# Stages behind a layer norm that open on raw inputs: four outputs before the norm is known, scale and bias put on the results

## The chip, the cores and the metric

The kernel runs on one NeuronCore of a Trainium2 chip. The metric is the device time of one execution in microseconds (us). TensorE (PE) multiplies, VectorE (DVE), ScalarE (ACT) and GpSimd (POOL) work on tiles in SBUF and in the PSUM banks; SyncE (SP) issues the DMAs.

## The reference, cut

Two transformer blocks of two layers each stand behind one another. Features are 1024 wide, there are 256 tokens in the first block and 272 (16 meta tokens ahead) in the second. Every layer norm is followed by the projections of the next part, which read its result `u` and nothing else:

```python
def layer_norm(x, g, b):
    mu = jnp.mean(xf, -1, keepdims=True)
    var = jnp.mean(jnp.square(xf - mu), -1, keepdims=True)
    return (xf - mu) * lax.rsqrt(var + EPS) * g + b
def swiglu(x, w_gate, w_up, w_down):
    return (jax.nn.silu(x @ w_gate) * (x @ w_up)) @ w_down
# first block, layer i (mixer 0 is RWKV-7, mixer 1 a gated delta net, "gdn")
    x = _layer_norm(DEEPNORM_ALPHA * x + (1 + ga1) * y, ln_g[i, 0], ln_b[i, 0])
    u = x * (1 + sc2) + sh2
    gate, up = jnp.split(u @ ffn_w_in[i], 2, axis=-1)
    y = (jax.nn.silu(gate) * up) @ ffn_w_out[i]
    x = _layer_norm(DEEPNORM_ALPHA * x + (1 + ga2) * y, ln_g[i, 1], ln_b[i, 1])
# second block, layer l
    h = layer_norm(ALPHA * h + 0.5 * swiglu(h, ffn1...), ln1_g[l], ln1_b[l])
    proj = h @ w_in[l]                      # SSD, forgetting and latent attention
    h = layer_norm(ALPHA * h + mix, ln2_g[l], ln2_b[l])
    h = layer_norm(ALPHA * h + 0.5 * swiglu(h, ffn2...), ln3_g[l], ln3_b[l])
```

Everything is fp32. The factor and summand on each norm's result that lead to `u` (g and b, and for the first block the modulation too) are kept as `lnc[:, n, 0, j]` and `lnc[:, n, 1, j]`, n the norm and j the tile of 128 features; `lnc[:, n, 2]` and `[3]` are those of the residual base (ALPHA times the norm's result).

## The kernel before

**Stages.** Behind the first mixer nine stages run: `STAGES = ("ffn", "gdn", "ffn", "ffn", "mixer", "ffn", "ffn", "mixer", "ffn")`, numbered 0 to 8, with norm n ahead of stage n (stage 3 opens the second block) and norm 9 at the end. Tiles are features by tokens: 8 tiles of 128 features, T = 256 or 272 columns. A ffn has 22 hidden tiles f, each with a gate output and an up output; outputs go to PSUM banks, gate f to bank 2(f%3), up f to the next one.

**Precision.** A product of fp32 numbers is made of three products on high and low parts (fp32r): high weight by high input, low weight by high input, high weight by low input. At 256 columns the high and low input stand side by side, so that one product 512 wide does two of them (f of 2 and more), and the halves are added behind it (`HALF`, `half_out`, L1929).

**Weights.** The weights come as slabs of 1 MB (16 blocks of 128x128) through a `ring` of 5 slots. ScalarE makes the high part into `high` (3 slots, L1446). Then the low part goes to `ring_low` by `ring - high`: on GpSimd (L2485) or, for hidden tiles of a ffn, on VectorE (`low_by_vector_engine`, L1909). `STAGE_AT[n]` (q0 below) is the stage's first slab.

**The norm.** `residual` (VectorE, ScalarE) takes the output projection's banks, adds them to the residual tiles `XAS` (L1829, L1832), subtracts a `shift` (half the mean over tiles that were early, kept in bank 3) into arena slot 9 (`less_shift`, L1810), and ScalarE squares them (L1434). The squares of tiles 1 to 6 go to PSUM banks 1 and 2, and VectorE adds them up (`add_square`, L1816). TensorE sums over features with matrix `con` into bank 4 (mean) and bank 5 (mean square). `norm` on VectorE (L1854 to L1901): variance, centering of XAS by pairs of tiles (`center`, L1858), ScalarE's square root, the reciprocal (L1868), then for each tile `normed_tile` (L1873), the whole input with scale and bias (L1888) and its low part (L1896, `input_low`); ScalarE's `norm_out` makes the input's high part (L1471, `input_high_ready`). Behind the eighth low part VectorE writes the residual base of eight tiles (L1901), which GpSimd sums (`base_sums`, L2501).

**The opening.** `first_four` on TensorE (all products have line L531) runs 4 outputs over k = 0 to 7, three products per output and k, 96 in all, and waits at each k for `input_high_ready` and `input_low`. In gdn and mixer stages these are the first four tiles of the convolution's channels, taken from banks 0 to 3 by VectorE's `convolve` (L2200, L2203) and ScalarE's silu (L1620, L1695); behind them stands a small product (`gdn_ba`, `dtf`) from which VectorE makes the decay rows (L2178 to L2214).

**GpSimd's order.** Its program for a stage is written out by hand:

```python
                weights_low(q0)
                weights_low(q0 + 1)
                eng.wait_ge(input_low, g.nth(input_low, DT))
                weights_low(q0 + 2)
                base_sums(To)
```

VectorE makes slab q0+3 at the start of `ffn`, and the high parts of q0+2 and q0+3 are first in ScalarE's `ffn` (in gdn and mixer stages q0+2 stands behind the norm).

## Time and profile before

| | us |
|---|---|
| median of 3 runs | 2307.1 |
| lowest, highest | 2302.41, 2310.05 |
| the profiled execution | 2305.64 |
| its span in the trace | 2303.7 |

In the span PE is busy 2112.9 us, DVE 1224.2, ACT 869.2 and POOL 708.9. The mean granted clock of TensorE is 0.958 of full speed. A row of the timeline shows the start, the duration with merged repeats (x2 is two instructions in a row), the engine and line, and in square brackets how long the engine had been idle and which instruction it was that ended this. Matmuls overlap, so durations of one are longer than the distance of two starts.

### The profile page before, as it was taken

The numbers are of one execution on the slowest core, as the hardware profiler recorded it, in microseconds if no ns is written. First come the engines' busy times: TensorE is split into PE (matmuls) and PEld (weight loads), VectorE is DVE, ScalarE is ACT, GpSimd is POOL, SyncE is SP. The second block draws the span as 40 slices with busy tenths as digits, with TensorE's granted clock in tenths as the row PEclk, the third lists the DMA queues.
The fourth block names the chain that finished last, engine by engine and source line by source line (L and its number), as shares of the span: only waits on it lengthen the run. The fifth ranks groups of instructions, "written<-read, shape, count | busy, mean of one in ns | idle before, by whom it ended". The sixth has DMA issues, their size and how long they took to land.

```text
span 2303.7 us, 40612 instructions
## 1 busy us (share of the span) xinstructions
PE 2112.9 (92%) x17634; PEld 1904.4 (83%) x17634; DVE 1224.2 (53%) x2205; ACT 869.2 (38%) x1258; POOL 708.9 (31%) x316
## 2 busy tenths in 40 slices
PE   4989988999988989999999898899999998989997
PEld 3867866889887867898999895699989997857897
DVE  6166445763673347653642666555264418457652
ACT  0442111454443223543433444343343334434543
POOL 0350001314573003126314560131561175304124
PEclk9998998999999899999999998899999998979999
DMA  8564442455343003554444340245435453304552
GB/s 330 220 274 148 149 163 75 150 184 188 141 147 128 2 1 128 188 196 166 160 170 180 131 147 19 92 169 180 167 145 179 169 177 108 119 19 147 184 191 83
DMA packets 49681, 340.43 MB, mean 148 GB/s; under 512 B 6368, under 2 KB 8416, under 8 KB 8672
## 3 DMA queue, kind: packets, MB, share of 16 engines
q1 hardware_dynamic: 49504, 337.84, 40.6%
q8 instruction: 139, 2.28, 0.4%
q14 instruction: 38, 0.31, 0.0%
HBM read 336.77 MB, written 1.05 MB: 147 GB/s over the span
## 4 chain that ended last, share of the span: by engine, by line
PE 81%; DVE 12%; ACT 3%; issue 2%; POOL 1%; DMA 1%; SPq 0%; ACTq 0%; POOLq 0%; DVEq 0%
PE bank L531 80%; POOL ring_low L2485 1%; DMA ada_ring<-ada 1%; DVE arena L1873 1%; DVE arena L1901 1%; PE bank L537 1%; DVE arena L1858 1%; ACT high L1446 1%; DVE small L1868 1%; DVE arena_parts L1896 1%; DVE arena L1888 0%; DVE ZZ L2082 0%; DVE small L2340 0%; DVE small L2451 0%; DVE acc L1963 0%
## 5 line engine op out<-in xcount | busy, mean ns | idle before, releaser
L531 PE MATMUL bank<-arena_parts,high 128*128 128x272 f32 (+2 forms) x4512 | 1026.4, 315 | 61.2 <-ACT arena_parts L1471 38.0
L531 PEld LDWEIGHTS bank<-arena_parts,high 128*128 128x128 f32 x4512 | 749.8, 191 | 111.6 <-issue 48.8
L531 PE MATMUL bank<-arena_parts,ring_low 128*128 128x272 f32 (+2 forms) x2736 | 782.1, 288 | 0.0
L1446 ACT ACTIVATE high<-ring 128x2048 fp32r<-128x2048 f32 x237 | 453.1, 1914 | 679.5 <-PE bank L531 593.5
L2485 POOL TENSOR_TENSOR ring_low<-ring,high 128x2048 fp32r<-128x2048 f32 x105 | 485.3, 4626 | 697.3 <-ACT high L1446 697.3
L531 PEld LDWEIGHTS bank<-arena_parts,ring_low 128*128 128x128 f32 (+1 forms) x2736 | 523.7, 191 | 1.0
L1909 DVE TENSOR_TENSOR ring_low<-ring,high 128x2048 fp32r<-128x2048 f32 x132 | 303.6, 2300 | 181.1 <-ACT high L1446 181.1
L531 PE MATMUL bank<-hidden_high,high 128*128 128x256 f32 (+1 forms) x1056 | 303.2, 287 | 0.0
L531 PE MATMUL bank<-hidden_low,high 128*128 128x256 f32 (+1 forms) x1056 | 301.1, 285 | 0.0
L531 PE MATMUL bank<-hidden_high,ring_low 128*128 128x256 f32 (+1 forms) x1056 | 300.1, 284 | 0.0
L2485 POOL TENSOR_TENSOR hidden_low<-arena,hidden_high 128x256 fp32r<-128x256 f32 (+1 forms) x132 | 111.8, 849 | 575.4 <-DVE hidden_high L1925 575.4
L531 PE MATMUL bank<-arena,ring 128*128 128x256 f32 (+2 forms) x992 | 230.6, 394 | 28.5 <-DVE arena L2158 7.8
L531 PEld LDWEIGHTS bank<-arena,ring 128*128 128x128 f32 (+1 forms) x992 | 192.9, 195 | 63.1 <-issue 11.4
L531 PEld LDWEIGHTS bank<-hidden_high,high 128*128 128x128 f32 x1056 | 199.0, 188 | 0.5
L531 PEld LDWEIGHTS bank<-hidden_high,ring_low 128*128 128x128 f32 x1056 | 198.9, 188 | 0.4
L531 PEld LDWEIGHTS bank<-hidden_low,high 128*128 128x128 f32 x1056 | 199.0, 188 | 0.0
L1829 DVE SCALAR_TENSOR_TENSOR acc<-bank,acc 128x272 f32<-128x272 f32 (+1 forms) x42 | 18.3, 436 | 177.8 <-PE bank L531 177.8
L531 PE MATMUL bank<-arena,con 64*64 64x64 f32 (+7 forms) x532 | 88.4, 336 | 15.7 <-issue 7.3
L531 PEld LDWEIGHTS bank<-arena,con 64*64 64x64 f32 (+4 forms) x532 | 45.4, 145 | 54.8 <-issue 24.8
L2501 POOL TENSOR_TENSOR acc<-arena 128x256 f32<-128x256 f32 (+1 forms) x20 | 26.9, 1345 | 194.9 <-PE bank L531 187.3
L1929 DVE TENSOR_TENSOR bank<-AZ,bank 128x256 f32<-128x256 f32 x60 | 25.8, 429 | 108.9 <-ACT AZ L1486 108.9
L2529 POOL TENSOR_TENSOR acc<-acc,ada_ring 128x1024 f32<-128x1024 f32 x21 | 49.6, 2363 | 99.4 <-ACT ada_ring L1458 97.4
(327 smaller groups left out, 2262.7 us busy)
## 6 DMA issues: line engine op xcount, KB each, us to landing
ring<-stream SPq DMA_DIRECT2D x269, 1024.0 KB, 4.8
ada_ring<-ada SPq DMA_DIRECT2D x48, 1024.0 KB, 6.2
con<-consts SPq DMA_DIRECT2D x1, 1542.5 KB, 11.1
con<-consts SPq DMA_DIRECT2D x1, 1040.0 KB, 7.2
arena<-xin SPq DMA_DIRECT2D x1, 1024.0 KB, 11.9
out<-arena SPq DMA_DIRECT2D x2, 512.0 KB, 2.9
prob_even<-consts SPq DMA_DIRECT2D x1, 320.0 KB, 11.4
par<-params SPq DMA_DIRECT2D x1, 272.5 KB, 9.7
```

Source lines behind the costliest of these rows:

```text
L531: ins = nc.tensor.matmul(o, l, r, start=start, stop=stop_, skip_group_check=True)
L537: ins = nc.tensor.transpose(o, x, con[0:rows, CC["ident"]:CC["ident"] + rows])
L1446: act(high[:, q % HIGHS], ring[:, s % RING], ACT.Copy).then_inc(a.sig(high_ready), 1)
L1858: nv.tensor_tensor(x, x, over_tiles(bank[4][:, 0:T], 2, T), ALU.subtract).then_inc(v.sig(vstep), 1)
L1868: nv.reciprocal(small[:, 2, 0:T], small[:, 1, 0:T]).then_inc(v.sig(vstep), 1)
L1873: nv.tensor_tensor(tl(9, j, T), tl(XAS, j, T, t0), small[:, 2, 0:T], ALU.mult).then_inc(v.sig(normed), 1)
L1896: nv.tensor_tensor(input_rest(j, T), tl(US, j, T, t0), input_high(STAGES[n], j, T).bitcast(F32), ALU.subtract).then_inc(v.sig(input_low), 1)
L1909: nv.tensor_tensor(ring_low[:, HL[q] % RING], ring[:, HL[q] % RING], high[:, q % HIGHS].bitcast(F32), ALU.subtract).then_inc(low_by_vector, 1)
L1929: nv.tensor_tensor(bank[b][:, 0:T], HALF[:, 0], bank[b][:, SEQ:], ALU.add).then_inc(v.sig(gate_added), 1)
L2485: ng.tensor_tensor(out, whole, part, ALU.subtract).then_inc(signal, 1)
L2501: ng.tensor_tensor(s_, first, tl(XAS, j, T, t0), ALU.add).then_inc(g.sig(sums_ready if j == 6 else pool_step), 1)
L2529: ng.tensor_tensor(acc[:, n % 2], acc[:, n % 2], w_k, ALU.add).then_inc(g.sig(ada_used if k % 2 else pool_step), 1)
```

## The change

Eight stages (`OPENED_RAW`, all but 3) open otherwise. Let x' be the tile less the shift (slot 9), g the gain, m the mean that remains in x', s the reciprocal of the deviation. With W the weight, W(g (x' - m) s + b) = s (W(g x') - m Wg) + Wb. So the four first outputs run on g x' (`raw_high` by ScalarE's `raw_tile`, `raw_low` by VectorE's `raw_rest`) before m and s are known. Four more columns per tile, the high and low parts of g and b (`raw_columns`), give Wg and Wb in the same products. The two norm sums (`mean_sum`, `square_sum`) move into the opening's k = 0. Then `scale_opened` on VectorE adds up the extra columns, puts -m Wg on the bank, multiplies by s, and (gdn and mixer) adds Wb. In a ffn, Wb of the gate is the bias of ScalarE's silu, and Wb of up is added in the hidden tile's instruction. The normed tiles are needed from the fifth output on (f=2), or by the small product.

With it go: `center` works on slot 9 with the mean in SBUF (`small[:, 0]`), one pair ahead of each pair of normed tiles; `less_shift` of tiles 4 to 7 reads the shift from SBUF (`small[:, 1]`); squares go to SBUF (`staged`) and not to banks 1, 2; the residual base is a function of its own and moves behind f=1 (ffn) or behind conv 2 (gdn, mixer), and in stage 3 to the start of `ffn`; ScalarE makes the high part of q0+2 before the first normed tile's high part and that of q0+3 in quarters behind tiles 2 to 5; GpSimd makes the low parts of q0 to q0+3 in a row.

```diff
+OPENED_RAW = (0, 1, 2, 4, 5, 6, 7, 8)
-    return STAGES[n] == "ffn" and HIGHS <= q - STAGE_AT[n] < HIGHS + FT
+    return STAGES[n] == "ffn" and HIGHS < q - STAGE_AT[n] < HIGHS + FT
...
+            def raw_four(n, tiles, T, signals):
+                for b in range(4):
+                    eng.wait_ge(*freed(b))
+                eng.wait_ge(raw_high_ready, pe.nth(raw_high_ready, 1))
+                eng.wait_ge(raw_low_ready, pe.nth(raw_low_ready, 1))
+                for k in range(DT):
+                    eng.wait_ge(raw_high_ready, pe.nth(raw_high_ready))
+                    eng.wait_ge(raw_low_ready, pe.nth(raw_low_ready))
+                    both, low = raw_both(n, k, T), raw_low(n, k, T)
...
+                    for b, (w_high, w_low) in enumerate(blocks):
+                        if k == 0 and b == 2:
+                            mean_sum(T)
+                        mm(bank[b][:, 0:T + 4], w_high, both, k == 0, False)
+                        m = mm(bank[b][:, 0:T + 4], w_low, both, False, k == DT - 1, hold=k == DT - 1)
+                    if k == 0:
+                        square_sum(T)
+                    if k < DT - 1:
+                        for b, (w_high, w_low) in enumerate(blocks):
+                            m = mm(bank[b][:, 0:T], w_high, low, False, False, hold=b == 3)
+                        m.then_inc(opened, 1)
+            def normal_tile():
+                eng.wait_ge(input_high_ready, pe.nth(input_high_ready))
+                eng.wait_ge(input_low, pe.nth(input_low))
...
         @block.scalar
-                    to = bank[1 + j % 2][:, 0:T] if j else square_sums(T)
+                    to = staged[:, j % 2, 0:T] if j else square_sums(T)
                     act(to, tl(9, j, T), ACT.Square).then_inc(a.sig(squared), 1)
+                    if raw:
+                        raw_tile(n, j, T)
                     if j >= 5 and highs:
                         weights_high(highs[j - 5])
...
+            def norm_out(n, T):
+                weights_high(STAGE_AT[n] + 2)
                 for j in range(DT):
                     eng.wait_ge(normed, a.nth(normed))
+                    act(input_high(STAGES[n], j, T), tl(9, j, T), ACT.Identity, ...)
+                    if raw and 2 <= j < 6:
+                        quarter_high(STAGE_AT[n] + HIGHS, j - 2)
...
         @block.vector
+            AFTER_FFN = ({5: (0, 1, 2), 6: (3, 4, 5, 6)}, ((), (), (7,)))
+            AFTER_MIXING = ({5: (0, 1), 6: (2,)}, ((3,), (4, 5), (6, 7)))
...
-                    nv.tensor_tensor(tl(9, j, T), tl(XAS, j, T, t0), bank[3][:, 0:T], ALU.subtract)
+                    shift = bank[3] if j < 4 else small[:, 1]
+                    nv.tensor_tensor(tl(9, j, T), tl(XAS, j, T, t0), shift[:, 0:T], ALU.subtract)
-                    nv.tensor_tensor(squares, squares, bank[1 + j % 2][:, 0:T], ALU.add)
+                    nv.tensor_tensor(squares, squares, staged[:, j % 2, 0:T], ALU.add)
...
-                    x = arena[:, XAS, 2 * q:2 * q + 2, t0:t0 + T]
-                    nv.tensor_tensor(x, x, over_tiles(bank[4][:, 0:T], 2, T), ALU.subtract)
+                    x = arena[:, 9, 2 * q:2 * q + 2, 0:T]
+                    nv.tensor_tensor(x, x, over_tiles(small[:, 0, 0:T], 2, T), ALU.add)
...
+            def scale_opened(b, T, signal, to_bias):
+                both = bank[b][:, T:T + 4].rearrange("p (a e) -> p a e", e=2)
+                nv.tensor_reduce(opening_cols[:, b], both, AX_X, ALU.add)
+                for i in range(1 if to_bias else 2):
+                    nv.scalar_tensor_tensor(out=product, in0=small[:, i, 0:T], scalar=opening_cols[:, b, i:i + 1], in1=product, ...)
+                nv.tensor_tensor(product, product, small[:, 2, 0:T], ALU.mult)
...
         @block.gpsimd
                 weights_low(q0)
                 weights_low(q0 + 1)
-                eng.wait_ge(input_low, g.nth(input_low, DT))
                 weights_low(q0 + 2)
+                weights_low(q0 + 3)
                 base_sums(To)
```

GpSimd, at the boundary to stage 0, before the change (`acc` rows are the sums of the residual base):

```order
L2501 TENSOR_TENSOR acc<-acc,arena 128x256 [waits pool_step]
L2485 TENSOR_TENSOR ring_low<-ring,high 128x2048 [waits weights_high_ready] x2
L2485 TENSOR_TENSOR ring_low<-ring,high 128x2048 [waits weights_high_ready,input_low]
L2501 TENSOR_TENSOR acc<-arena 128x256 [waits residual_base_ready]
```

and with it:

```order
L2688 TENSOR_TENSOR acc<-acc,arena 128x256 [waits pool_step]
L2672 TENSOR_TENSOR ring_low<-ring,high 128x2048 [waits weights_high_ready] x4
L2688 TENSOR_TENSOR acc<-arena 128x256 [waits residual_base_ready]
L2688 TENSOR_TENSOR acc<-acc,arena 128x256 [waits pool_step] x2
```

The third slab no longer waits for `input_low`, and a fourth one, which was VectorE's, stands behind it.

VectorE at the same place, from the last residual tile on, before (L1832 the last tile, L1810 `less_shift`, L1868 the reciprocal):

```order
L1832 SCALAR_TENSOR_TENSOR arena<-bank,mod,arena 128x256
L1810 TENSOR_TENSOR arena<-arena,bank 128x256
L1854 TENSOR_TENSOR small<-bank,small 128x256
L1858 TENSOR_TENSOR arena<-arena,bank 128x2x256
L1864 SCALAR_TENSOR_TENSOR small<-bank,small 128x256
L1858 TENSOR_TENSOR arena<-arena,bank 128x2x256
L1868 RECIPROCAL small<-small 128x256
L1873 TENSOR_TENSOR arena<-arena,small 128x256 x2
L1888 TENSOR_SCALAR arena<-arena,lnc 128x256 x2
L1858 TENSOR_TENSOR arena<-arena,bank 128x2x256 x2
L1896 TENSOR_TENSOR arena_parts<-arena,arena_parts 128x256 x2
```

and with the change (L1932 is `raw_rest`, L2003 `center`, L2013 `normed_tile`):

```order
L1966 SCALAR_TENSOR_TENSOR arena<-bank,mod,arena 128x256
L1944 TENSOR_TENSOR arena<-arena,small 128x256
L1932 SCALAR_TENSOR_TENSOR arena_parts<-arena,lnc,arena_parts 128x256
L1991 TENSOR_TENSOR small<-small,bank 128x256
L1932 SCALAR_TENSOR_TENSOR arena_parts<-arena,lnc,arena_parts 128x256 x2
L1996 SCALAR_TENSOR_TENSOR small<-bank,small 128x256
L1932 SCALAR_TENSOR_TENSOR arena_parts<-arena,lnc,arena_parts 128x256 x2
L2003 TENSOR_TENSOR arena<-arena,small 128x2x256
L2008 RECIPROCAL small<-small 128x256
L2013 TENSOR_TENSOR arena<-arena,small 128x256 x2
L2031 TENSOR_SCALAR arena<-arena,lnc 128x256 x2
L2003 TENSOR_TENSOR arena<-arena,small 128x2x256
```

Five `raw_rest` instructions now stand among them, one `center` less stands ahead of the reciprocal, and `less_shift` and `center` read `small`, not a bank.

## Rows read from the trace of the kernel before

**Rows 1.** The page, busy time (share) xinstructions, and the chain by engine.

```profile
PE 2112.9 (92%) x17634; PEld 1904.4 (83%) x17634; DVE 1224.2 (53%) x2205; ACT 869.2 (38%) x1258; POOL 708.9 (31%) x316
...
PE 81%; DVE 12%; ACT 3%; issue 2%; POOL 1%; DMA 1%; SPq 0%; ACTq 0%; POOLq 0%; DVEq 0%
```

**Rows 2.** PE's waits: instruction <- releaser: us in total, times, longest.

```profile
PE bank L531 <- ACT arena_parts L1471: 38.0, 9, 4.3
...
PE bank L531 <- ACT arena L1695: 8.8, 4, 2.4
...
PE bank L531 <- POOL ring_low L2485: 7.2, 8, 1.1
```

**Rows 3.** Timeline of PE: start, us, instruction [idle before <-releaser], first norm.

```profile
406.53 0.59 PE L531 MATMUL bank<-acc,con 128*128 128x256 f32 x2
...
413.02 0.55 PE L531 MATMUL bank<-arena_parts,high 128*128 128x256 f32 x1 [4.15 <-ACT arena_parts L1471]
...
427.31 0.47 PE L531 MATMUL bank<-arena_parts,high 128*128 128x512 f32 x1 [0.81 <-POOL ring_low L2485]
...
444.16 0.39 PE L531 MATMUL bank<-arena_parts,high 128*128 128x512 f32 x1
```

**Rows 4.** Windows: us, PE busy (matmuls), granted clock, DMA share, GB/s.

```profile
413.02:417.20 4.18, 4.18 (x19) 0.50 0.53 198
417.20:427.30 10.10, 9.30 (x79) 1.00 0.35 128
...
609.30:615.30 6.00, 5.98 (x28) 0.50 0.01 3
```

**Rows 5.** Timeline of DVE, first norm, its first and last steps.

```profile
411.71 0.76 DVE L1873 TENSOR_TENSOR arena<-arena,small 128x256 f32<-128x256 f32 x2
...
420.19 0.76 DVE L1896 TENSOR_TENSOR arena_parts<-arena,arena_parts 128x256 fp32r<-128x256 f32 x2
```

**Rows 6.** Lines (ns min/median/max); timeline of DVE and POOL behind the first norm.

```profile
L1901 DVE TENSOR_SCALAR arena<-arena,lnc x72: 396/423/4868, 420.9 to 2114.3; 128x256 f32<-128x256 f32 x40, 128x272 f32<-128x272 f32 x32
...
L2189 DVE SCALAR_TENSOR_TENSOR arena<-arena x21: 411/428/4730, 647.7 to 1950.6; 12x272 f32<-12x272 f32 x14, 8x256 f32<-8x256 f32 x7
...
L2180 DVE RECIPROCAL arena<-arena x3: 1740/1841/1842, 640.7 to 1941.9; 12x272 f32<-12x272 f32 x2, 8x256 f32<-8x256 f32 x1
...
L1810 DVE TENSOR_TENSOR arena<-arena,bank x80: 409/421/439, 395.9 to 2290.2; 128x256 f32<-128x256 f32 x48, 128x272 f32<-128x272 f32 x32
...
421.51 6.46 DVE L1901 TENSOR_SCALAR arena<-arena,lnc 128x256 f32<-128x256 f32 x6
...
422.38 4.79 POOL L2485 TENSOR_TENSOR ring_low<-ring,high 128x2048 fp32r<-128x2048 f32 x1 [25.87 <-ACT high L1446]
```

**Rows 7.** Timeline of POOL and DVE, residual phase behind the first feed-forward.

```profile
594.52 9.17 POOL L2485 TENSOR_TENSOR ring_low<-ring,high 128x2048 fp32r<-128x2048 f32 x2 [2.61 <-ACT high L1446]
...
595.25 0.42 DVE L1810 TENSOR_TENSOR arena<-arena,bank 128x256 f32<-128x256 f32 x1
```

**Rows 8.** Prices: POOL's group (busy, mean ns), and lines (ns min/median/max).

```profile
L2485 POOL TENSOR_TENSOR ring_low<-ring,high 128x2048 fp32r<-128x2048 f32 x105 | 485.3, 4626 | 697.3 <-ACT high L1446 697.3
...
L1446 ACT ACTIVATE high<-ring x237: 1892/1917/1927, 356.7 to 2272.1; 128x2048 fp32r<-128x2048 f32 x119
...
L1909 DVE TENSOR_TENSOR ring_low<-ring,high x132: 2273/2287/2781, 427.9 to 2228.8; 128x2048 fp32r<-128x2048 f32 x132
...
L2203 DVE SCALAR_TENSOR_TENSOR XX<-bank,par,XX x72: 479/482/486, 626.2 to 698.7; 128x255 f32<-128x255 f32 x24, 128x254 f32<-128x254 f32 x24, 128x253 f32<-128x253 f32 x24
...
L2366 DVE COPY TC<-bank x6: 148/160/165, 1387.8 to 2001.8; 128x12 f32<-128x12 f32 x4, 16x12 f32<-16x12 f32 x2
```

**Rows 9.** Timeline of DVE and PE in the gdn stage.

```profile
617.12 7.11 DVE L1901 TENSOR_SCALAR arena<-arena,lnc 128x256 f32<-128x256 f32 x8
...
642.46 4.47 DVE L2182 TENSOR_TENSOR arena<-arena 8x256 f32<-8x256 f32 x1
...
655.14 0.58 PE L531 MATMUL bank<-arena_parts,high 128*128 128x256 f32 x1 [6.45 <-ACT arena L1620]
```

More of the change, by code:

```diff
@@ L1066, in _ @@
             out_projection("rwkv_out", 0, 8, lambda k: tl(5, k), SEQ)
-            norm(SEQ)
-            ffn("ffn_in", "ffn_in", "ffn_out", 0, SEQ, FT)
-            norm(SEQ)
-            first_four("gdn", [("gdn_in", 0, n) for n in range(4)], SEQ, [told(b, "vector") for b in B4])
+            ffn(0, "ffn_in", "ffn_in", "ffn_out", 0, SEQ, FT)
+            raw_four(1, [("gdn_in", 0, n) for n in range(4)], SEQ, [told(b, "vector") for b in B4])
             prev[0:4] = ["scalar"] * 4
@@ L1237, in mixer @@
             def mixer(l):
-                first_four("mixer", [("mix_in", l, n) for n in range(4)], T, [told(b, "vector") for b in B4])
+                raw_four(4 + 3 * l, [("mix_in", l, n) for n in range(4)], T, [told(b, "vector") for b in B4])
                 prev[0:4] = ["scalar"] * 4
@@ L1477, in ffn, with result_out @@
+                if not raw:
+                    weights_high(STAGE_AT[n] + HIGHS)
+            def result_out(n, T):
+                for j in range(DT):
+                    eng.wait_ge(normed, a.nth(normed))
+                    act(tl(US, j, T, xview(T)), tl(9, j, T), ACT.Identity, bias=lnc[:, n, 1, j:j + 1],
+                        scale=lnc[:, n, 0, j:j + 1]).then_inc(a.sig(output_ready), 1)
             def ffn(n, T):
                 q0 = STAGE_AT[n]
-                weights_high(q0 + 2)
@@ L1815, in add_square @@
                         eng.wait_ge(*added["squares"])
-                    nv.tensor_tensor(squares, squares, bank[1 + j % 2][:, 0:T], ALU.add).then_inc(v.sig(square_added), 1)
+                    nv.tensor_tensor(squares, squares, staged[:, j % 2, 0:T], ALU.add).then_inc(v.sig(square_added), 1)
                     added["squares"] = v.last
@@ L1872, in normed_tile @@
                     eng.wait_ge(*centers[j // 2])
-                    nv.tensor_tensor(tl(9, j, T), tl(XAS, j, T, t0), small[:, 2, 0:T], ALU.mult).then_inc(v.sig(normed), 1)
+                    nv.tensor_tensor(tl(9, j, T), tl(9, j, T), small[:, 2, 0:T], ALU.mult).then_inc(v.sig(normed), 1)
                     return v.last
                 if n == len(STAGES):
-                    centers += [center(2), center(3)]
+                    centers += [center(1), center(2), center(3)]
                     for j in range(DT):
```

304 lines of the change are left out of this document (210 added, 94 removed).

## The prediction

> **What bounds the kernel now.** I read the page's busy shares and its chain first: TensorE is busy 92% of the span and carries 81% of the chain, VectorE 12% [rows 1]. So TensorE's idle time is what an edit can win. The list of TensorE's waits names the part this change aims at: nine waits for ScalarE's normed inputs (L1471), 38.0 us, and eight for GpSimd's `ring_low` (L2485), 7.2 us [rows 2]. The timeline of the first layer norm shows both: the first product of the next stage starts at 413.02 after 4.15 us idle, the third output (f=2) only at 427.31, f=5 at 444.16, so 5.62 us per output from there on [rows 3]. The windows show the clock: after the gap 4.2 us ran at 0.50 of full speed, the lower of the two levels (1.2 GHz), and 6.0 us at the second norm [rows 4]. Ten norms run, one before each of nine stages and one at the end; eight stages (all but stage 3) get the new opening.
>
> **What is freed on TensorE.** The opening is 96 products before and after. The gap ends; 96 products at the warm 0.118 us (79 records took 9.30 us in the third window [rows 4]) are 11.4 us, the four passes of norm sums now inside it 0.9. From the end of the product that closes the projection (407.1 [rows 3]) TensorE would stand before f=2 at 419.5 and not at 427.31: 7.8 us, if all inputs are there. The extra four columns (64 products 260 wide for 256) are 0.1 us per stage. Over eight stages some 60 us are on offer.
>
> **What TensorE then waits for.** f=2, and in gdn and mixer stages the small product behind the four outputs, needs the normed tiles. VectorE makes them in the order of before: its chain ran from 411.71 to 420.9 [rows 5]. Now two raw tails more stand ahead of the variance and two behind it, 0.4 us each, less the second `center`: the reciprocal ends at 412.9 and not 411.7, and with one more `center` per pair the chain would end at 422.9. TensorE, waiting for it in f=2, keeps some 3.9 of the 7.8.
>
> **The mechanism on which I decide.** VectorE instructions whose tensor inputs all lie in SBUF stop while GpSimd runs. L1901, scale and bias of a tile in SBUF, takes 0.42 us as a rule and 4.87 at most [rows 6]: six of them, due 2 us, took 6.46 from 421.51 because GpSimd's `weights_low` ran 422.38 to 427.17. A scalar_tensor_tensor on SBUF tiles waited likewise (L2189, 0.43 as a rule, 4.73 at most), and a tensor_tensor (L2182, 4.47 us for 8x256) [rows 6, 9]. The reciprocal does not: L2180 stays between 1.74 and 1.84. Nor does L1810, one input in PSUM: never over 0.439 in 80 calls, though GpSimd ran two weight slabs beside it from 594.52 [rows 6, 7]. Before, the norm's critical chain was clear of GpSimd: the third `weights_low` waited for the eighth `input_low`, and up to there VectorE's shift, centering and square sums had PSUM inputs.
> The Trainium skill, SBUF — State Buffer, "SBUF: two separate sides", states it as a rule: VectorE in a two-port mode or with two SBUF inputs and GpSimd share a port pair by an exclusive lock held for the whole instruction. L1901 (4.87) and L1810 (0.439) agree; it is a rule against this change.
>
> The change drops the wait for `input_low`, gives GpSimd a fourth slab in the opening, and takes the PSUM operands away from `less_shift` for tiles 4 to 7, `add_square` and `center`. Prices: a slab is 4.63 us on GpSimd, its high part 1.9 on ScalarE, its low part 2.29 on VectorE [rows 8].
> - Third slab. ScalarE makes its high part right after the square root (1.9 us), before VectorE's reciprocal (1.74) and the instruction ahead of it have ended. GpSimd gets the port first, from about 412.1 to 416.7; the first `normed_tile`, ready at 412.9, starts at 416.7: 3.8 us.
> - Fourth slab. ScalarE's quarters end after tile 5 (about 424.7); VectorE is in tiles 6 and 7: 4.6 us more.
> So `input_low` 8 comes at 422.9 + 3.8 + 4.6, and 0.5 for the quarters between ScalarE's tiles: 431.8, not 420.9. f=2 has idled 1, 2 and 6 us between its tiles by then; its up half runs 432.2 to 435.0 (before: to 432.9, 427.31 + 5.62).
> - Handover. VectorE scales the first gate and up after that: for each a reduce, a scalar_tensor_tensor of PSUM (0.48 [rows 8]) and a product (0.42), then two products of 0.48 and the silu: 3.5 us. The reduce of four columns has no row. Its bounds are 0 and 0.48; I take 0.12, by the copies of 12 PSUM columns, 0.16 [rows 8]. f=3 starts at 435.5 (before 432.9), f=4 at 441.6 (438.5), and, since eight `residual_base` (2.7), a 2.29 slab and the halves stand before tile 2, f=5 at 448.6 (444.16 [rows 3]). From there TensorE is the bound, so the stage keeps +4.4. At 272 columns no halves are added and an output takes longer on TensorE: of the 4.4 some 2.1 stay (stage 5).
>
> **After a feed-forward** the residual phase is hit too. GpSimd's slab starts at 594.52, and VectorE's `less_shift(6)` at 595.25 [rows 7]; with the raw tile ahead of ScalarE's high part the slab starts at 595.0. Now an SBUF instruction, `less_shift(6)` waits to 599.6; square 6, and behind it high part and slab q0+1, come 4 us later, and that slab (602.8 to 607.4) lies over `less_shift(7)`. Squares and sums are 3.7 us late. TensorE, which has the square sum behind its first eight products, idles 3 us there; then come the two slabs of above. By the same sum: stage 6 (ffn) +3.7; stage 3, without raw opening but with the new order, +4.5.
>
> **gdn (stage 1).** TensorE's tile 10 waited 6.45 us to 655.14 for a ScalarE silu behind VectorE's conv 6, which stood behind the decay rows (L2182 at 642.46 is one) [rows 9]. So VectorE's chain sets that time. Its `input_low` 8 moves from 617.1 [rows 9] by the late squares 3.7, raw tails and centers 2.2, and the two slabs 3.8 + 4.6: +14.3. Then four openings add 1.45 each to the convolutions (+5.8); `residual_base` no longer meets a slab (4.87 - 0.42 = -4.4); the decay rows meet other slabs (-4: one of their two stops of 4.0 and 4.3 falls away; 0 if neither does). Sum +11.7. **Mixers (4, 7).** The decay rows have slack there. What binds is bank 3 coming free, behind three opened convolutions, the base and a fourth: VectorE's chain +12, openings +5.8, base -4.4, less the old waits for L1695 (8.8 us in the two [rows 2], 4.4 each) and 0.5 of slack: +8.5 each. The final norm: one more `center` behind the reciprocal, +0.6 to 1.
>
> **Sum.** Stages 0, 2, 8: 3 x 4.4 = 13.2; stage 5: 2.1; stage 6: 3.7; stage 3: 4.5; stage 1: 11.7; stages 4, 7: 17; the end 0.8: **+53**. The clock gives nothing back at the boundaries counted here, since f=2 waited for GpSimd's slab in the trace of before, not for the slow products. The profiled execution took 2305.64 us for a span of 2303.7; its time plus 53 is 2358.6. The median of the three runs is 1.5 above it, so I take 2359.
>
> **The rivals.**
> 1. *The port does not decide* (faster). If GpSimd's slabs fall where VectorE is in reciprocals or PSUM work, or the stop is shorter than L1901's, what is left is the clean order. f=5 of stage 0 then starts at 440.2, 3.9 us before the old one; 3.9 x 3 for stages 0, 2, 8, stage 5 -6, stage 6 -6.5, stages 3 and 9 0, gdn and mixers +3 and +2.3 x 2 by the openings. Sum -17 with old clocks, down to -34 where the half-speed stretches of the gdn and mixer openings also go (up to 6.0 [rows 4]): 2272 to 2290. For it: the idle time of [rows 2] is real. Against it: the one L1901 of 4.8 us that each of the nine `residual_base` runs holds.
> 2. *Some of the stops miss.* The race at 595.0 against 595.25 is 0.3 us wide. If `less_shift(6)` wins in all five boundaries behind a feed-forward, some 3.5 x 5 = 17 fall away: 2341. If besides the fourth slab came after `input_low` 8 (ScalarE 7 us later), 8 x 3 more: about 2315.
> 3. *More idle brings more half-speed time.* The 6 us gap in f=2 and 3 us in k=0 are of the length that stood before 4.2 and 6.0 us at half speed [rows 3, 4]; where products, not VectorE, bind behind it, that is 1 to 2.5 us for each of nine: 2358 + 15 = 2373.
>
> **How the numbers follow.** Forecast with its variants 2 (first) and 3: 0.76. The strong form of rival 2, around 2315: 0.07. Rival 1: 0.14. The rest, 0.03, is within 0.3%, which is about what a measurement of this kernel can tell from no change (2300 to 2314), and half of rival 2's strong form lies beside its edge: 0.06 for no change in all, 0.80 slower. I leave out rival 1 and the farthest sums, so the range is 2308 to 2378. Faster by over 0.3%: 0.14.
>
> **What would show it.** In the profile after: TensorE's list without the 4.2 us waits before the opening, and in their place waits inside f=2 and the small products for VectorE's `input_low`, 5 to 7 us at the longest; the first `normed_tile` of most norms at 4 us and another one at 5 instead of 0.43; `less_shift` up to 4.5 us; GpSimd's slab starting while the reciprocal runs. It is wrong if these instructions keep 0.42 us beside a running slab, if the tile-6 `less_shift` stays short, or if gdn's tile 10 starts less than 8 us later against its projection's end.

## The result and the profile after

| | before | with the change |
|---|---|---|
| median, us | 2306.88 (4 runs, 2302.41 to 2310.05) | 2384.73 (4 runs, 2384.56 to 2385.05) |
| ratio | | 1.0344, 95% interval 1.0319 to 1.0369 |
| span of the profiled execution | 2303.7 | 2382.8 |

3.4% slower: the direction of the forecast, and outside its range (2308 to 2378). The forecast was +53 us; the profiled spans differ by 79.1.

The page of the changed kernel, busy times and the chain of work that ended last, beside [rows 1]:

```profile
PE 2130.4 (89%) x17634; PEld 1919.7 (81%) x17634; DVE 1352.5 (57%) x2386; ACT 900.2 (38%) x1362; POOL 730.0 (31%) x322
...
PE 57%; DVE 12%; issue 2%; ACT 2%; ACTq 0%; DVEq 0%
```

VectorE is busy 128 us more. A stopped instruction counts as busy. With GpSimd's opening slabs left out (`no_open_lows` and its control, below) VectorE is busy 1238.8 us in the changed kernel and 1183.2 in the one before. So some 56 us are more work (among it 64 raw tails of 0.49 us), and the time that goes with the slabs rose from 41 to 114 us. The waits of TensorE (instruction <- releaser: us in all, times, longest), beside [rows 2]:

```profile
PE bank L568 <- DVE arena_parts L2039: 63.5, 23, 5.3
...
PE bank L568 <- ACT arena L1810: 23.5, 4, 9.2
PE bank L568 <- DVE arena L1966: 19.8, 6, 5.4
```

The nine waits of 4.2 us ahead of the openings are down to one (stage 3, which opens as before). In their place stand waits for VectorE's low parts of the input (L2039), in f=2 and in the small products; for the mixers' silu (L1810); and, not forecast, for the last residual tile (L1966).

The timeline of VectorE and GpSimd behind the first norm shows the mechanism on which the forecast decided, beside [rows 5]. First VectorE, then GpSimd:

```profile
419.49 1.75 DVE L2008 RECIPROCAL small<-small 128x256 f32<-128x256 f32 x1
421.27 4.48 DVE L2013 TENSOR_TENSOR arena<-arena,small 128x256 f32<-128x256 f32 x2
...
433.43 4.60 DVE L2031 TENSOR_SCALAR arena<-arena,lnc 128x256 f32<-128x256 f32 x1
...
420.52 4.61 POOL L2672 TENSOR_TENSOR ring_low<-ring,high 128x2048 fp32r<-128x2048 f32 x1 [15.67 <-ACT high L1540]
432.83 5.05 POOL L2672 TENSOR_TENSOR ring_low<-ring,high 128x2048 fp32r<-128x2048 f32 x1 [7.70 <-ACT high L1566]
```

GpSimd's third slab starts while the reciprocal runs (which keeps its 1.75), and the first normed tile is free only when the slab ends; the fourth slab stops a whole tile (L2031) for 4.2 us. So it is in all eight raw norms: the first normed tile takes 4.0 to 4.5 us there, the whole tile 4.6. The residual phase ahead of norm 4 (behind a feed-forward) shows what the forecast had wrong:

```profile
1319.32 0.44 DVE L1944 TENSOR_TENSOR arena<-arena,small 128x272 f32<-128x272 f32 x1
1319.68 9.56 DVE L1950 TENSOR_TENSOR acc<-acc,XX 128x272 f32<-128x272 f32 x2
1329.16 1.73 DVE L1932 SCALAR_TENSOR_TENSOR arena_parts<-arena,lnc,arena_parts 128x272 fp32r<-128x272 f32 x4
1330.81 0.43 DVE L1966 SCALAR_TENSOR_TENSOR arena<-bank,arena 128x272 f32<-128x272 f32 x1
...
1319.61 9.33 POOL L2672 TENSOR_TENSOR ring_low<-ring,high 128x2048 fp32r<-128x2048 f32 x2 [5.50 <-ACT high L1540]
...
1331.30 1.27 PE L568 MATMUL bank<-arena,con 128*128 128x272 f32 x2 [4.45 <-DVE arena L1966]
```

`less_shift(6)` (L1944) just gets ahead of the slab, so ScalarE squares the tile and makes the next high part at once, and slab q0+1 follows q0 without a gap. Two `add_square` (L1950) stand still, 9.56 us for 0.87 us of work; the raw tails and the last residual tile, which TensorE waits for, stand behind them.

I set the two traces side by side stage by stage. The mark is the sixth of the eight products `bank<-acc,con` ahead of each norm (at norm 0 it starts at 405.02 in the kernel before, 1.5 us ahead of the 406.53 of [rows 3]); it stands at the same place among the 17634 products in every kernel. Stage n runs from the mark of norm n to that of norm n+1. Differences to the profiled execution of before, us:

| kernel | head | 0 | 1 | 2 | 3 | 4 | 5 | 6 | 7 | 8 | end |
|---|---|---|---|---|---|---|---|---|---|---|---|
| forecast | 0 | 4.4 | 11.7 | 4.4 | 4.5 | 8.5 | 2.1 | 3.7 | 8.5 | 4.4 | 0.8 |
| the change | 8.4 | 3.1 | 10.5 | 2.9 | 6.6 | 15.1 | 3.1 | 8.4 | 17.0 | 3.4 | 0.6 |
| changed_again | 3.8 | 3.2 | 10.6 | 2.9 | 6.6 | 19.3 | 2.7 | 8.2 | 16.8 | 3.3 | 0.6 |
| no_open_lows | 3.6 | -5.3 | -4.6 | -5.2 | -0.9 | 4.4 | -7.0 | -7.7 | -1.5 | -5.4 | 0.6 |
| no_open_lows_before | 1.7 | -0.9 | -12.7 | -1.2 | -0.9 | 0.5 | -0.4 | -1.5 | -2.9 | -1.3 | 0.0 |
| before_sbuf_operands | 6.6 | 0.2 | 3.1 | 0.3 | 2.1 | -1.9 | 0.0 | 1.2 | 1.7 | 0.1 | 0.0 |
| before_third_slab_early | 5.9 | 4.5 | -4.4 | 4.2 | 5.1 | 1.6 | 3.9 | 3.9 | -2.4 | 4.5 | 0.0 |
| changed_psum_squares | 1.9 | 2.9 | 7.3 | 2.7 | 4.0 | 15.6 | 2.7 | 5.0 | 10.2 | 3.1 | 0.6 |
| third_waits_again | 0.6 | 2.1 | 1.3 | 1.9 | 2.8 | 10.6 | 1.9 | 7.7 | 5.0 | 2.2 | 0.6 |
| second_slab_behind_shift | 2.8 | 3.1 | 7.1 | 2.9 | 4.7 | 16.3 | 3.4 | 5.3 | 13.7 | 3.4 | 0.6 |
| third_high_ahead | 3.1 | -0.6 | 15.8 | 0.0 | 7.3 | 22.9 | -0.7 | 8.3 | 24.0 | -0.3 | 0.6 |
| slabs_in_quarters | -0.4 | 2.6 | 7.5 | 2.5 | 4.3 | 15.3 | 2.3 | 4.5 | 12.1 | 2.3 | 0.6 |
| open_behind_mixers_3 | 9.6 | -4.4 | 0.8 | -4.4 | 0.9 | 1.9 | -5.7 | 0.8 | 0.4 | -4.4 | 0.6 |

Stages 0, 2, 3, 5, 6, 8 are feed-forwards, 1 is gdn, 4 and 7 are mixers. The head is the time ahead of the first mark. Its difference scatters from execution to execution: at the first residual sum of norm 0 (394.88 before), ahead of which no edit acts, the eighteen traces lie between -0.8 and +8.5. So some times below are compared without the heads too. Only where the third slab runs ahead of the first mark is a part of the head the edit's own: 1.1 us in open_behind_mixers_3, 3.9 in third_high_ahead.

### The profile page after: what moved, and what is told of

Same layout as the page of the kernel before. It is cut to its first block, busy times and chain, and to the rows that moved or that the text cites. A ratio compares the mean times of both kernels' runs of the same rounds, so it can differ in the third digit from the quotient of the medians.

```text
span 2382.8 us, 41142 instructions
## 1 busy us (share of the span) xinstructions
PE 2130.4 (89%) x17634; PEld 1919.7 (81%) x17634; DVE 1352.5 (57%) x2386; ACT 900.2 (38%) x1362; POOL 730.0 (31%) x322
## 4 chain that ended last, share of the span: by engine, by line
PE 57%; DVE 12%; issue 2%; ACT 2%; ACTq 0%; DVEq 0%
PE bank L568 56%; DVE acc L1950 2%; DVE arena L2031 2%; DVE arena L2384 1%; PE bank L574 1%; DVE arena_parts L2039 1%; DVE arena L2013 1%; DVE bank L2057 1%; DVE arena_parts L1932 0%; DVE small L2008 0%; DVE XX L2384 0%; DVE arena L2003 0%; DVE arena L2047 0%; DVE small L2638 0%; DVE small L2527 0%
## 5 line engine op out<-in xcount | busy, mean ns | idle before, releaser
L568 PE MATMUL bank<-arena_parts,high 128*128 128x272 f32 (+4 forms) x4512 | 1042.4, 318 | 102.1 <-DVE arena_parts L2039 63.5
L568 PE MATMUL bank<-arena_parts,ring_low 128*128 128x272 f32 (+4 forms) x2736 | 786.1, 290 | 0.0
L2672 POOL TENSOR_TENSOR ring_low<-ring,high 128x2048 fp32r<-128x2048 f32 x111 | 515.2, 4644 | 691.6 <-ACT high L1540 628.8
L1540 ACT ACTIVATE high<-ring 128x2048 fp32r<-128x2048 f32 x229 | 438.4, 1914 | 638.4 <-PE bank L568 551.9
L2065 DVE TENSOR_TENSOR ring_low<-ring,high 128x2048 fp32r<-128x2048 f32 x126 | 290.6, 2306 | 172.7 <-ACT high L1540 172.7
L2688 POOL TENSOR_TENSOR acc<-arena 128x256 f32<-128x256 f32 (+1 forms) x20 | 14.9, 746 | 317.9 <-PE bank L568 194.0
L568 PE MATMUL bank<-arena,con 64*64 64x64 f32 (+7 forms) x512 | 82.1, 334 | 31.7 <-DVE arena L1966 19.8
L1950 DVE TENSOR_TENSOR acc<-acc,XX 128x256 f32<-128x256 f32 (+1 forms) x60 | 76.0, 1267 | 59.6 <-ACT XX L1513 57.2
```

The lines of the kernel that those rows point to most:

```text
L568: ins = nc.tensor.matmul(o, l, r, start=start, stop=stop_, skip_group_check=True)
L1540: act(high[:, q % HIGHS], ring[:, s % RING], ACT.Copy).then_inc(a.sig(high_ready), 1)
L1950: nv.tensor_tensor(squares, squares, staged[:, j % 2, 0:T], ALU.add).then_inc(v.sig(square_added), 1)
L2065: nv.tensor_tensor(ring_low[:, HL[q] % RING], ring[:, HL[q] % RING], high[:, q % HIGHS].bitcast(F32), ALU.subtract).then_inc(low_by_vector, 1)
L2672: ng.tensor_tensor(out, whole, part, ALU.subtract).then_inc(signal, 1)
```

## The experiments

**Is it the slabs at all?** The low parts of the opening are left out, in the changed kernel and in the one before.

```diff
-                weights_low(q0)
-                weights_low(q0 + 1)
-                weights_low(q0 + 2)
-                weights_low(q0 + 3)
+                for q in range(q0, q0 + 4):
+                    eng.wait_ge(high_ready, q + 1)
+                    rest(low_stub[:, ...one column...], low_stub[:, 0:1], low_stub[:, 0:1], low_by_gpsimd)
```

In both kernels TensorE takes the high parts in place of the low parts left out, in as many products of the same size.

> The changed kernel, with GpSimd's four weights_low of each opening (q0 to q0+3) left out: GpSimd only signals, and TensorE multiplies by the high part in place of the low one, in as many products of the same size. Theory A (GpSimd's slabs stop VectorE's SBUF instructions): no normed_tile, whole tile or add_square over 1 us is left, and the time falls from 2384.7 to between 2280 and 2300. Rival B (VectorE simply has more to do: raw tails, scaling of the opened banks, one more center): the slabs are not what is waited for, the time stays above 2350.

> The kernel before, with its three weights_low of each opening left out in the same way: the control for the run above. Both theories: TensorE's eight waits for ring_low (7.2 us) and the stopped L1901 go, the rest stays: 2290 to 2302 against 2307. What this run and the one above differ in is what the change gives or costs where no slab stands in VectorE's way: theory A says -5 to -20, rival B +30 or more.

Measured: 2276.36 us for the changed kernel and 2286.04 for the one before, beside a run of before at 2304.82. So GpSimd's slabs cost the changed kernel 108 us and the old one 19. Both times lie some 4 us below the ranges expected; rival B falls. Against the expectation one `add_square` behind each feed-forward is still stopped in the changed kernel (2.1 to 2.7 us), by a slab that does not belong to the opening. The line of the normed tiles in the changed kernel without slabs (ns min/median/max):

```profile
L2016 DVE TENSOR_TENSOR arena<-arena,small x80: 407/420/443, 416.5 to 2269.1; 128x256 f32<-128x256 f32 x48, 128x272 f32<-128x272 f32 x32
```

With the slabs its longest was 4735 ns. The difference of the two rows of the table is what the new opening is worth where nothing stops VectorE: -4 to -4.4 in stages 0, 2 and 8, -6.6 and -6.2 in stages 5 and 6, but +8.1 in gdn and +3.9 and +1.4 in the mixers, where VectorE's own chain sets the time and `scale_opened` lengthens it. In all some -10 us, not the 60 that stood idle. The two kernels differ in one more thing: in the control VectorE still makes slab q0+3 (2.29 us). In stage 3, which opens alike in both, the difference is 0.0, so that this slab is not seen to matter there.

**One part alone in the kernel before: the operands.**

```diff
+                    shift = bank[3] if j < 4 else small[:, 1]
-                    nv.tensor_tensor(tl(9, j, T), tl(XAS, j, T, t0), bank[3][:, 0:T], ALU.subtract)
+                    nv.tensor_tensor(tl(9, j, T), tl(XAS, j, T, t0), shift[:, 0:T], ALU.subtract)
-                    to = bank[1 + j % 2][:, 0:T] if j else square_sums(T)
+                    to = staged[:, j % 2, 0:T] if j else square_sums(T)
```

> The kernel before, with only the operands moved: less_shift of tiles 4 to 7 reads the shift from SBUF, and ScalarE's squares go to SBUF, where add_square reads them. The instructions are as many and as long. Theory A: behind each feed-forward (norms 1, 3, 4, 6, 7) two add_square or less_shift take 4 us and more beside the slabs q0 and q0+1; behind a mixer nothing moves. Each of the five boundaries loses 4 to 7: 2325 to 2342. Rival B: no operand matters, 2303 to 2311.

Measured: 2319.3 against 2304.82, in neither range. The head of this execution is 6.6 late, the five boundaries cost 6 in all (stages 1, 3, 4, 6, 7 of the table). The timeline, VectorE and then GpSimd, ahead of norm 4, shows why so little:

```profile
1300.29 4.63 DVE L1819 TENSOR_TENSOR acc<-acc,XX 128x272 f32<-128x272 f32 x1 [0.68 <-ACT XX L1431]
1307.21 0.44 DVE L1835 SCALAR_TENSOR_TENSOR arena<-bank,arena 128x272 f32<-128x272 f32 x1 [2.29 <-PE bank L533]
1307.68 1.95 DVE L1813 TENSOR_TENSOR arena<-arena,small 128x272 f32<-128x272 f32 x1
...
1300.02 9.31 POOL L2489 TENSOR_TENSOR ring_low<-ring,high 128x2048 fp32r<-128x2048 f32 x2 [5.08 <-ACT high L1448]
```

The stop is there, 4.63 us. But VectorE had idle time ahead of the last residual tile (2.29 us are left of it), which swallows one stop. A second, of `less_shift(7)` (1.95 for 0.44), is followed by a wait of TensorE for the last square, 1.7 us. In the changed kernel two stops and four raw tails stand ahead of the last residual tile, and 4.45 us come out at TensorE.

**One part alone: the third slab early.**

```diff
+                if n < len(STAGES):
+                    weights_high(STAGE_AT[n] + 2)
                 for j in range(DT):
                     eng.wait_ge(normed, a.nth(normed))
...
                 weights_low(q0 + 1)
-                eng.wait_ge(input_low, g.nth(input_low, DT))
                 weights_low(q0 + 2)
```

> The kernel before, with the high part of slab q0+2 made right behind the norm's square root, and GpSimd's low part of it with no wait for input_low: this part of the change alone. Theory A: the first normed_tile of nine norms takes 4.2 us in place of 0.43, the gap on TensorE grows from 4.2 to 8 us; 0.9 us of the wait for ring_low and the stopped L1901 come back: +2 to +4 per norm, 2325 to 2343. Rival B: the slab is ready earlier and nothing else moves, 2298 to 2307.

Measured: 2332.57, as theory A said (2326.7 without the head). VectorE's and GpSimd's lines behind the first norm:

```profile
417.59 5.08 DVE L1872 TENSOR_TENSOR arena<-arena,small 128x256 f32<-128x256 f32 x2
...
417.62 4.77 POOL L2484 TENSOR_TENSOR ring_low<-ring,high 128x2048 fp32r<-128x2048 f32 x1 [15.33 <-ACT high L1446]
```

TensorE's waits for the normed inputs went from 38.0 to 55.0 us. Each feed-forward stage loses 3.9 to 5.1; stages 1 and 7 gain 4.4 and 2.4. `residual_base` is no longer stopped (4.8 us before) in this kernel, which would shorten VectorE's chain there; that it is the reason was not tested by itself.

**Undo that part in the changed kernel, and move single slabs.**

```diff
                 weights_low(q0 + 1)
+                eng.wait_ge(input_low, g.nth(input_low, DT))
                 weights_low(q0 + 2)
```

> The changed kernel with GpSimd's wait for the eighth input_low put back ahead of slab q0+2 (q0+3 behind it). Theory A: no normed_tile and no whole tile over 1 us is left, input_low 8 comes 8 us earlier; TensorE then waits 4.6 us for slab q0+2, where before it came in 0.9; the two add_square of 4 us behind feed-forwards stay. 2345 to 2362. Theory A2 (the slab has to run at some time, and only moves what is late): 2370 or more.

Measured: 2342.29, 2.7 below theory A's range. No normed or whole tile is stopped, and 42 us come back (35 without the heads), although TensorE now waits for the slab itself:

```profile
PE bank L568 <- POOL ring_low L2672: 37.3, 5, 7.9
```

So the two slabs q0+2 and q0+3 cost less on TensorE's own path (37.3 us in all) than as two stops in VectorE's chain.

```diff
                 weights_low(q0)
+                if n in (1, 3, 4, 6, 7):
+                    eng.wait_ge(centered, g.nth(centered, DT))
                 weights_low(q0 + 1)
```

> The changed kernel; behind feed-forwards (stages 1, 3, 4, 6, 7) GpSimd waits for the eighth less_shift before slab q0+1, which TensorE needs only from k=4 on. Theory A: the second stopped add_square goes (4.1 us), the first stays and is hidden in VectorE's idle time ahead of residual tile 7; q0+1 now meets the last raw tail, under 1 us. 4 stages x 4 and 2 for stage 3: 2362 to 2370. Rival C (the residual phase is late for another reason: the raw tails and ScalarE's raw tiles): 2380 or more.

Measured: 2368.72, inside the range. The second `add_square` is free, but q0+1 with q0+2 right behind it now stops a raw tail (2.85 us) and the pair `center` (5.13), so that a part of the gain is lost to another stop. The head of this execution is 5.6 us shorter than that of the change, so only some 10 of the 16 us are the edit's.

```diff
             def norm_out(n, T):
...
-                weights_high(STAGE_AT[n] + 2)
+                if n in (1, 3, 4, 6, 7):
+                    weights_high(STAGE_AT[n] + 2)
...
             def first_highs(n):
-                for q in range(2):
+                for q in range(3):
                     weights_high(STAGE_AT[n] + q)
```

> The changed kernel; behind mixers (stages 0, 2, 5, 8) ScalarE makes the high parts of q0, q0+1 and q0+2 ahead of the norm, so that GpSimd's third slab runs during the output projection. Theory A: the first normed_tile of 4.1 us falls to 0.43 in these four norms; the whole tile of 4.6 (slab q0+3) stays. 3 to 3.8 us in each: 2370 to 2374. If TensorE, not VectorE, set the time there, nothing moves: 2383 to 2386.

Measured: 2386.98: nothing gained, outside both ranges. In stages 0, 2, 5, 8 the 3 us came (3.1 to -0.6, 2.9 to 0.0, 3.1 to -0.7, 3.4 to -0.3), and stages 1, 4 and 7 lost 5 to 8 each. The next run shows the place.

**All slabs placed.** Both edits, and a wait for the eighth `input_low` ahead of q0+3 (behind mixers) or q0+2 (behind feed-forwards).

> The changed kernel with the slabs placed where VectorE has PSUM operands or is idle: the two edits above, and GpSimd waits for the eighth input_low ahead of q0+3 (stages 0, 2, 5, 8) or q0+2 (the others). Theory A: with all slabs left out the changed kernel took 2276; what stays is TensorE's wait for a slab that starts at input_low 8, 3 to 5 us in five stages: 2292 to 2312, about the time of before. If the sum of single effects doesn't hold (a slab moved meets other VectorE work in the handover), 2320 to 2345.

Measured: 2332.05, the second branch. The third slab, now early, runs under the residual phase behind the mixer, and stops an `add_square` there; TensorE waits for the bank that VectorE has not read (VectorE, GpSimd, TensorE ahead of norm 5):

```profile
1488.40 3.99 DVE L1951 TENSOR_TENSOR acc<-acc,XX 128x272 f32<-128x272 f32 x2 [4.27 <-ACT XX L1513]
...
1487.03 4.51 POOL L2673 TENSOR_TENSOR ring_low<-ring,high 128x2048 fp32r<-128x2048 f32 x1 [2.91 <-ACT high L1540]
...
1493.93 0.79 PE L568 MATMUL bank<-arena,ring 128*128 128x272 f32 x1 [4.58 <-DVE arena L1967]
```

> slabs_placed with the third high part behind the fourth square in place of ahead of the first, so that the slab meets less_shift of tile 5 in a stretch where VectorE has idle time, and not add_square of tile 1 (3.0 us, and 4.6 us of TensorE's wait for a bank behind it). Theory A: the loss that showed at the end of stages 1, 4 and 7 in slabs_placed, some 5 us each, goes: 2312 to 2320 against 2332. If the loss came from elsewhere: 2330 or more.

Measured: 2323.92, 8 us less, 4 above the range. With the high part behind the fourth square the slab stops a later `add_square` (4.1 us). TensorE still waits for the residual tile behind it: 3.37, 3.38, 2.78 and 3.25 us in the four norms behind mixers (VectorE, GpSimd, TensorE at norm 0):

```profile
402.53 4.53 DVE L1953 TENSOR_TENSOR acc<-acc,XX 128x256 f32<-128x256 f32 x1 [0.84 <-ACT XX L1513]
...
402.26 4.51 POOL L2675 TENSOR_TENSOR ring_low<-ring,high 128x2048 fp32r<-128x2048 f32 x1 [4.96 <-ACT high L1542]
...
408.85 2.07 PE L568 MATMUL bank<-acc,con 128*128 128x256 f32 x4 [3.37 <-DVE arena L1969]
```

**What is a stop bound to?** Each slab as four instructions.

```diff
+                    for i in range(4):
+                        p_ = slice(4 * i, 4 * i + 4)
+                        rest(ring_low[:, HL[q] % RING, p_], ring[:, HL[q] % RING, p_], high[:, q % HIGHS, p_].bitcast(F32), low_by_gpsimd if i == 3 else g.sig(pool_step))
```

> The changed kernel with each of GpSimd's four opening slabs written as four instructions of 4 blocks. Theory A1 (VectorE is held for the instruction that runs, and gets its turn behind it): no VectorE instruction above is stopped for more than 1.3 us, the longest normed_tile is near 1.6; but up to four are stopped per slab, so most of the time is lost again: 2350 to 2375. Theory A2 (GpSimd keeps the port from one instruction to the next while it has work): stops of 4 us as before, 2383 to 2390.

Measured: 2359.28, in the range of theory A1. VectorE and GpSimd behind the first norm:

```profile
412.47 2.24 DVE L2013 TENSOR_TENSOR arena<-arena,small 128x256 f32<-128x256 f32 x2
414.63 2.69 DVE L2031 TENSOR_SCALAR arena<-arena,lnc 128x256 f32<-128x256 f32 x2
...
411.72 5.45 POOL L2672 TENSOR_TENSOR ring_low<-ring,high 128x512 fp32r<-128x512 f32 x4 [15.27 <-ACT high L1540]
```

The two engines take turns: a VectorE instruction gets in behind each quarter, and the first is stopped by 0.4 us and the next three by 1.0 to 1.1 in place of one by 4. The sum stays near the slab's length: 3.4 us for this slab, where the whole one took 3.7. Ahead of norm 4 the stops add up to 6.7 us in place of 8.6. The kernel is 25.5 us faster than the change, 16.7 without the heads. So smaller instructions spread the cost and here saved a quarter of the loss; they don't take it away.

**The operands of before, in the changed kernel.**

```diff
-                    to = staged[:, j % 2, 0:T] if j else square_sums(T)
+                    to = bank[1 + j % 2][:, 0:T] if j else square_sums(T)
-                    shift = bank[3] if j < 4 else small[:, 1]
+                    shift = bank[3]
-                    nv.tensor_tensor(squares, squares, staged[:, j % 2, 0:T], ALU.add)
+                    nv.tensor_tensor(squares, squares, bank[1 + j % 2][:, 0:T], ALU.add)
```

> The changed kernel with the operands of before in the residual phase: squares in PSUM banks 1 and 2, the shift in bank 3; TensorE waits for six add_square ahead of bank 1 and for the eighth less_shift ahead of bank 3. Theory A: no add_square over 0.5 us; of the two stops of 4.4 and 4.1 behind a feed-forward the raw tails (SBUF only) take one over. 3 to 6 us less in stages 1, 4, 6, 7 and 2 in stage 3: 2360 to 2372. If the slabs stop the raw tails for as long as they stopped the squares: 2380 or more.

> The changed kernel once more. If the 8.4 us ahead of the first norm are scatter between executions, this profile has between 0 and 8 there and the stages are late by 70 as before: 2375 to 2385. If they belong to the new program: 8 to 9 us there again and 2384 to 2386.

Measured: 2361.71, and for the changed kernel once more 2385.1 (2383.77 and 2386.42). Of the 23 us, 16.7 are left without the heads. VectorE, then GpSimd, ahead of norm 4:

```profile
1305.24 0.44 DVE L1950 TENSOR_TENSOR arena<-arena,bank 128x272 f32<-128x272 f32 x1
1305.59 0.99 DVE L1956 TENSOR_TENSOR acc<-acc,bank 128x272 f32<-128x272 f32 x2
1306.50 8.44 DVE L1938 SCALAR_TENSOR_TENSOR arena_parts<-arena,lnc,arena_parts 128x272 fp32r<-128x272 f32 x2
...
1305.29 9.36 POOL L2677 TENSOR_TENSOR ring_low<-ring,high 128x2048 fp32r<-128x2048 f32 x2 [3.91 <-ACT high L1546]
```

This is the cleanest view of the rule: beside the same slab, two `add_square` with one input in PSUM take 0.99 us together, and the next instruction, all in SBUF, stands. The stops have moved on to two raw tails (7.5 us in place of 8.6), but TensorE's wait for the last residual tile falls from 4.45 to 2.07 us in stages 4, 6 and 7 and from 5.38 to 3.15 in stage 1. 3.2 to 6.8 us come back in stages 1, 6 and 7 and 2.6 in stage 3, and none in stage 4, whose time differs by 4 even between two executions of the change (15.1 and 19.3).

**A version from this.** The new opening pays behind mixers (0, 2, 5, 8), and there only if the slabs keep clear.

```diff
+OPENED_RAW = (0, 2, 5, 8)
...
+                if n in OPENED_RAW:
+                    weights_low(q0 + 2)
+                    eng.wait_ge(input_low, g.nth(input_low, DT))
+                    weights_low(q0 + 3)
+                else:
+                    eng.wait_ge(input_low, g.nth(input_low, DT))
+                    weights_low(q0 + 2)
```

> The new opening in stages 0, 2, 5, 8 only (behind a mixer), the old one behind feed-forwards. In the four: the high part of q0+2 behind the fourth square, GpSimd's low part of it at once, q0+3 behind the eighth input_low. In the five others the order of before, centering from PSUM again, and q0+1 behind the eighth less_shift. Theory A: stages 0, 2, 8 keep the -3.2 to -4.0 and stage 5 the -5.3 that they had in slabs_placed, without its stopped add_square ahead of them (6 us each); the others stay within 1 of before. 2288 to 2298 against 2307. If a stage opened raw doesn't pay even with its slabs placed: 2303 to 2312.

> The kernel with the new opening behind mixers only, and the PSUM operands in every residual phase. Theory A: stages 0, 2, 5, 8 at -3.5, -4, -5.5, -4 against before, the others at 0: 2285 to 2297 against 2304 to 2307, faster by 0.4 to 0.8%. If the opening's gain is eaten by TensorE's waits for the banks that the squares hold: 2300 to 2308.

> slabs_placed_2 with the PSUM operands of the run above. Theory A: the third slab no longer stops add_square behind mixers (4.1 us, of which some 2 showed) and the first one none behind feed-forwards: 2308 to 2320 against 2324. If the stops were hidden in VectorE's idle time: 2320 to 2328.

Measured: 2308.28 (ratio 1.0015, 0.9996 to 1.0035), 2311.58 (1.002, 1.0003 to 1.0036) and 2325.9 (beside 2323.92 of slabs_placed_2). None kept theory A's range; the first and the third lie in the range of the rival named with them, the second above both. In the first the third slab, started behind the fourth square, stops an `add_square` by 4.1 us in each of the four norms as in slabs_placed_2, and TensorE waits as there (12.8 us in all). PSUM operands alone gave nothing: the same slab now stops the instruction that writes the low parts of the raw columns (L1940 of that kernel, 3.8 us), and TensorE waits 11.3 us. So the last version starts the slab ahead of the squares, where VectorE reads PSUM:

```diff
-                    if j == 3 and raw:
-                        weights_high(STAGE_AT[n] + 2)
...
-                for q in range(2):
+                for q in range(3):
                     weights_high(STAGE_AT[n] + q)
```

> open_behind_mixers_2 with the third high part ahead of the squares (as in slabs_placed), so that GpSimd's slab runs while VectorE's less_shift and add_square read PSUM, and is over before most raw tails. Theory A: no VectorE instruction over 1.5 us is left in norms 0, 2, 5 and 8 ahead of the hand-over; stages 0, 2, 5, 8 at -3 to -5.5 against before: 2290 to 2303, between the same and 0.6% faster. If ScalarE's third high part, 1.9 us ahead of the first square, holds the squares and the raw tiles up instead: 2305 to 2313.

Measured: 2289.46 (6 runs, 2284.8 to 2301.47) against 2306.26, ratio 0.9928, 95% interval 0.9906 to 0.9949. It is faster than both kernels. No stop over 1.5 us is left around the four raw norms, and their stages keep -4.4, -4.4, -5.7, -4.4. The page of its profiled execution (span 2299.7, the longest of its six, with a head of +9.6):

```profile
PE 2112.4 (92%) x17634; PEld 1906.2 (83%) x17634; DVE 1220.3 (53%) x2288; ACT 884.2 (38%) x1310; POOL 724.9 (32%) x320
```

VectorE is as busy as before [rows 1], with 83 instructions more.

## Why the forecast's direction was right, and where it failed

- **Freed on TensorE, and taken back.** Right in kind. With no slab in the way the opening gave 4 to 6.6 us in a feed-forward; rival 1 had said 3.9 and 6. For gdn it had said a loss of 3, the runs showed 8.
- **The mechanism.** Right. The first normed tile takes 3.6 to 4.1 us more (forecast 3.8), a whole tile 4.2 (forecast 4.6), in all eight raw norms; reciprocal and PSUM work untouched. In the change every reciprocal began ahead of its slab; in the open_behind_mixers kernels 24 began while a slab ran and took 1.74 to 1.85 us as well.
- **The hand-over and stages 0, 2, 8.** Forecast +4.4, measured +3.1, 2.9, 3.4. The reduce of four columns took 0.15 us, near the 0.12 that I took. Stage 5: 2.1 and 3.1.
- **After a feed-forward: the step that failed.** I had GpSimd win the race and stop `less_shift(6)`, so that square 6 and slab q0+1 came later: squares and sums 3.7 us late, 3 us of it at TensorE. `less_shift(6)` won in all four raw norms behind a feed-forward (1319.32 against 1319.61; the lead was 0.24 to 0.29 us) and stayed at 0.44 us, which the prediction had named as a sign that it is wrong. I had counted such a win as a gain of 3.5 per boundary (rival 2). It is none: the slabs then run back to back and stop two `add_square`, 4.4 and 4.1 us. I had `add_square` on the list of instructions that lost their PSUM operand and never walked it past the slabs. The term is 8.6 us of stop in each of stages 1, 4, 6, 7, and a wait of TensorE for the last residual tile of 5.4 us in stage 1 and 4.45 in the other three. Stage 6: 3.7 forecast, 8.4 measured; mixers 8.5 each, 15.1 and 17.0 measured. changed_psum_squares took 3.2 to 6.8 of it back in three of the four.
- **The mixers' rest.** no_open_lows minus its control leaves +3.9 and +1.4 for the opening alone; with the stops of norm and residual phase VectorE's chain is later by more than I took: TensorE waits 12.3 and 11.2 us for the silu (L1810) in stages 4 and 7, where it waited 4.0 and 4.7 before (L1695). Which part of stage 4 is scatter stays open: two executions of the same kernel gave 15.1 and 19.3.
- **gdn.** 11.7 forecast, 10.5 measured, but not for my reasons alone: 4.8 more in the residual phase were offset elsewhere in the stage. I had read the decay rows' two stops as 4.0 and 4.3; the 4.3 (L2189 at 4.73) belongs to a mixer. In the gdn stage they were 1.75 and 4.06 (2.02 and 4.47 us, L2178 and L2182), and one of 2.9 is left (3.27, L2360): 3 us less, where I took 4.
- **The head.** 8.4 us of the 79.1 lie in the head, 3.8 in the change's second profile. I had given the head no term, and took a single profile's time as the base. TensorE was busy 7.1 us longer with the same products there: 51.2 us of this head ran at the lower level of the granted clock and 34.1 of that of before. In the second profile it was 41.0 us, and 1.2 us busier; the rest of the scatter stays open. So does the reason why the change's four runs agree within 0.5 us with such a head. Without the heads the miss is 17.7 us (70.7 against 53): stages 3, 4, 6 and 7 are 21.9 over the forecast, the rest 4.2 under it.
- **Clock.** Rival 3 had some weight. TensorE's busy time for the same 17634 products rose by 17.5 us: 7.1 in the head, 0.9 to 1.0 in each of stages 0, 2, 3, 5 and 8, 2.5 in stage 6, 1.4 and 4.1 in the mixers, and 2.0 less in gdn. In the mixers it need not show in the time, since VectorE's chain is waited for behind it. An instance is the 5.7 us at 0.50 behind the wait ahead of norm 4's sums:

```profile
1331.30:1337.00 5.70, 5.70 (x19) 0.50 0.00 0
```

(The columns are those of [rows 4].)

## What to carry to other kernels

Before an instruction loses its PSUM operand, or a GpSimd instruction is started earlier, list every VectorE instruction that can run beside it, and walk both outcomes of each race: a win may only hand the stop to the next instruction. A long GpSimd instruction beside such work cost VectorE nearly its full length here, and most of it still when it was cut in four; place it under PSUM reads, reciprocals or idle time, and check what waits behind that idle time. An opening that hides a norm pays where TensorE is the bound behind it (feed-forwards here), not where VectorE's chain is (gdn, mixers).
